# Weight products placed a unit at a time beside the heads of four attentions, and repeated products in the norms

## The chip, the cores and the metric

The kernel runs on one core of a Trainium2 chip. The metric is the device time of one execution in microseconds. All tensors are float32.

## The reference

A block with batch 1, 256 tokens and width 1,024, then a second one on its output. The first has two layers: latent attention (mla) and a full attention with a distance bias (moba, which with 256 tokens has a single key block), each followed by a residual sum, layer norm and a feed-forward layer with a three-tap convolution (width 2,816), again with residual sum and norm. The second has an attention mixer of two kinds (swa: a window with a sink and a bias table; fgt: a decaying attention), whose joined heads are gated, and a linear recurrence. Every normed input is scaled and shifted by a modulation vector that is computed from c. Cut to what matters:

```
for i in (0, 1):                                   # first block
    mod = silu(c) @ mod_w[i] + mod_b[i]            # 6 x 1024
    y = mixer_i(x * (1 + scale) + shift)           # mla, then moba: 8 heads of 128
    x = layer_norm(4 ** .25 * x + gate * y)
    y = conv_ffn(x * (1 + scale2) + shift2)
    x = layer_norm(4 ** .25 * x + gate2 * y)
for i in (0, 1):                                   # second block
    mod = silu(c_2) @ ada_w[i] + ada_b[i]          # 3 x 1024
    h = rmsnorm(x) * (1 + scale) + shift
    y = (concat(swa(h), fgt(h)) * silu(gate)) @ w_out   or   rglru(h)
    x = x + gate * y
out = rmsnorm(x)
```

## The kernel before, in words

Five engines each have a hand-written list of instructions, which meet in counted semaphores. Features lie on partitions and tokens in the free dimension, in tiles of 128 x 256.

**Weights.** `weight_stream` lists the chunks (128 x 2,048 elements, 1 MB) in the order of use. The sync engine fetches them into the ring `raw` of three chunks. A chunk is two *units* of 1,024 columns. For every unit ScalarE writes the rounded half `w_hi`, and then VectorE the remainder `w_lo = raw - w_hi`; both rings hold six units. The functions `ahead(u)` on both engines do this up to unit u, and `product(key)` does it up to five units beyond a chunk and then waits until TensorE has used the chunk (`w_used`). Each product is then three matmuls, hi x hi, hi x lo and lo x hi (`feature_product` with features out, `token_product` with tokens out). A unit is 24 matmuls of 256 columns or 12 of 512.

**Modulation.** GpSimd fetches 88 row blocks of `mod_w` and `ada_w_2` (`modulation`) into two slots `modraw`. VectorE's `modulate(n)` multiplies n of them by an element of silu(c) and adds them to an accumulator of 2,048 or 1,024 columns. `fold` on TensorE turns a finished accumulator, and on VectorE sums it.

**Attention.** Function `attention` on three engines. In turn t of before, TensorE makes the scores of head t, transposes the probabilities of head t-2 and makes the value product of head t-3. VectorE takes the maximum of head t's scores with mask or bias (L1622, L1624) and the shift (L1633), then the reciprocal of head t-1 (L1642) and o_lo of head t-4 (L1646), and at some turns a modulation step (L1404). ScalarE makes the exponentials of head t (L1073, L1075), normalises head t-1 (L1085, L1087), copies the transposed probabilities probT of head t-2 (L1096) and o_hi of head t-3 (L1102). No weight product stands in an attention; the next units are converted until the rings are full. Projections end before an attention begins, and the product with the output weights (`out_projection`, 8 units) begins after it. `swa` and `fgt` put two heads into one tile (`pair`).

**Norms.** Behind an output product, VectorE adds the four blocks to x (`block_sum`, L1476), VectorE and ScalarE make the statistics and scale x, TensorE turns it (`norm_turns`, L587) first for tokens 0 to 127 and then for the rest, and ScalarE evicts with the modulation. The norm between the first and the second block (layer 3 followed by rms norm, `layer_then_rms_norm`) needs the gain and offset rows, which `ln_rows(3)` has fetched into vv in the sixth iteration of the second feed-forward layer. GpSimd clears vv for swa's and fgt's values behind that norm (L495), beside VectorE's scaling of x (L1603).

Of the kernel before, what the change touches and what calls it, by code (L numbers as in the profile page):

```python
# [16 lines left out]
P = 128  # L17
D = 1024
KT = D // P
# [39 lines left out]
VZ = 10  # L59
# [56 lines left out]
def weight_stream(w):  # L116
# [35 lines left out]
    for part in range(3):  # L152
        for m in range(4):
            cols(("moba_in", part * 4 + m), w["moba_w_in"][0], part * 1024 + m * 256)
    rows2("moba_o", w["moba_w_o"][0])
    ffn(1)
    ain = w["attn_w_in_2"][0]
    cols(("a_kv", 0), ain, 512)
    cols(("f", 0), ain, 2304, 8, 2)
# [46 lines left out]
def build(nc, w, consts, out):  # L206
# [29 lines left out]
    with ExitStack() as ctx:  # L236
# [62 lines left out]
        def vtile(t, n, a=0, b=P):  # L299
# [15 lines left out]
        modacc = [of[:, :] if g in (3, 5, 7) else kk[:, 8 * S:12 * S] if g == 2 else  # L315
                  vv[:, 8 * S:12 * S] if g == 10 else modsum[:, :] for g in range(NG)]
# [13 lines left out]
        gain_row = [bias[:, 4 * S:8 * S], bias[:, 4 * S:8 * S], vv[:, 0:D], vv[:, 0:D]]  # L330
        offset_row = [vv[:, 0:D], kk[:, 8 * S:12 * S], vv[:, D:2 * D], vv[:, D:2 * D]]
# [57 lines left out]
        turn_keys = [("moba_in", i) for i in range(12)]  # L389
        turn_keys += [("a_kv", 0), ("f", 0)] + [(n, m) for n in ("a_q", "b_q", "b_k", "b_v") for m in range(2)]  # L390
        turn_keys += [("a_gate", m) for m in range(4)] + [("xr", m) for m in range(4)]
        turn_keys += [("l_gate", m) for m in range(4)]
        turn_of = {key: n for n, key in enumerate(turn_keys)}

# [51 lines left out]
        def _(pool):  # L446
# [31 lines left out]
            modulation(4 * KT, 7 * KT - 1)  # L478
            for h in range(2, HEADS):
                alibi_table(h)  # L480
                if h in (4, 7):
                    n = 7 * KT - 1 + (h - 4) // 3
                    modulation(n, n + 1)
            modulation(7 * KT + 1, 8 * KT)
            pool.wait_ge(sem("head_out"), 16)
            pool.wait_ge(sem("x_updated"), 2)
# [6 lines left out]
            modulation(8 * KT, 8 * KT + VZ)  # L493
            pool.wait_ge(sem("x_updated"), 4)
            pool.memset(vv[:, :], 0.0).then_inc(sem("vv_zero"), 1)  # L495
            modulation(8 * KT + VZ, len(mods))

# [8 lines left out]
        def _(pe):  # L506
# [18 lines left out]
            def columns_chunk(key, dst, a, width=256, e=None, heads=None):  # L525


                u0 = unit0(*key)
                step = min(width, P)
                for u in (u0, u0 + 1):  # L530
                    start_unit(u)
                    for k in range(4):
                        kt = 4 * (u - u0) + k
                        if e is not None:
                            pe.wait_ge(sem("h_ready"), 8 * e + kt + 1)
                        if heads is not None:
                            pe.wait_ge(sem("o_ready"), heads[kt])
                        for f in range(width // step):
                            at = k * width + f * step
                            ins = feature_product(dst[0:step, f * S:(f + 1) * S], u,  # L540
                                                  lambda r: r[:, at:at + step], tiles(a[0], kt, kt + 1),
                                                  tiles(a[1], kt, kt + 1), kt == 0 and f == 0, kt == KT - 1)
                    if u == u0:
                        ins.then_inc(sem("w_used"), 1)
                return ins

            def end_chunk(ins):
                ins.then_inc(sem("w_used"), 1)

            def turn(key):  # L550

                n = turn_of[key]
                if n >= 4:
                    pe.wait_ge(sem("turn_read"), n - 3)
# [1467 lines left out]
```

## Time and profile before

| | us |
|---|---|
| median of 3 runs (983.44 to 989.82) | 984.64 |
| the profiled execution | 988.01 |
| its span | 986.2 |
| TensorE matmul busy | 848.5 (86%) |
| VectorE busy | 743.2 (75%) |
| ScalarE busy | 518.5 (53%) |
| GpSimd busy | 74.4 (8%) |
| mean granted TensorE clock | 0.942 of 2.4 GHz |

The profiled execution took 1.8 us more than its span. Matmuls overlap in the records, so TensorE's work is read from the distance of their starts. Stages by the start of their products: mla's projections to 103, its attention to 135, mla_o to 158, first feed-forward layer 165 to 357, moba's projections to 437, attention to 466, moba_o to 489, second feed-forward layer 495 to 692, the second block's projections 711 to 769, swa and fgt to 821, gates and attn_o to 872, recurrence to the end.

### The profile page before, as it was taken

The page shows a single profiled execution, that of the slowest core. Times are in us where ns is not written, and L with a number is a line of the kernel's source. Part 1 is how long each engine was busy: PE and PEld are TensorE (multiplying, and loading weights), DVE is VectorE, ACT ScalarE, POOL GpSimd, SP SyncE. Part 2 cuts the span into 40 slices and gives each one's busy share as a digit, 9 for nine tenths or more (in the row PEclk, how much of TensorE's full clock was granted, in tenths as well). Part 3 has the DMA queues.
Part 4 walks back from the last instruction along what each step waited for, and adds up shares of the span by engine and source line. Part 5 has one row for each costly group of instructions (what it writes and reads, how often), then busy time and mean ns, then how long its engine had stood idle before and what let it go on. Part 6 is the DMA issues. An engine that isn't in the chain of part 4 may idle for free.

```text
span 986.2 us, 14678 instructions
## 1 busy us (share of the span) xinstructions
PE 848.5 (86%) x5608; PEld 775.1 (79%) x5608; DVE 743.2 (75%) x1153; ACT 518.5 (53%) x891; POOL 74.4 (8%) x118
## 2 busy tenths in 40 slices
PE   0387898999999989987899999999499789888946
PEld 0277677999999979976798998998399668778935
DVE  3889768787878778886688867767778655779684
ACT  0345656545445474447473535544555666464961
POOL 1000010010000000113000040000100000000100
PEclk9888999999999989997989999999699899999878
DMA  8877744778797739985457799865198511656411
GB/s 326 282 232 273 242 161 142 253 248 307 274 326 264 273 120 347 378 316 182 149 159 288 257 219 330 268 223 178 69 290 285 171 43 65 207 172 198 171 43 43
DMA packets 122677, 216.29 MB, mean 219 GB/s; under 512 B 12235, under 2 KB 97975, under 8 KB 115440
## 3 DMA queue, kind: packets, MB, share of 16 engines
q1 hardware_dynamic: 106828, 134.79, 40.7%
q0 software_dynamic: 12960, 72.46, 21.4%
q10 hardware_dynamic: 2820, 8.11, 2.5%
q8 instruction: 45, 0.74, 0.3%
q14 instruction: 24, 0.20, 0.1%
HBM read 214.18 MB, written 1.15 MB: 218 GB/s over the span
## 4 chain that ended last, share of the span: by engine, by line
PE 58%; DVE 21%; ACT 10%; DMA 5%; issue 5%; SPq 0%; DVEq 0%; ACTq 0%
PE bank L515 11%; PE bank L516 11%; PE bank L517 11%; PE bank L521 6%; PE bank L523 6%; PE bank L522 6%; DVE w_lo L1374 5%; DVE modsum L1404 3%; DMA raw<-in_ffn_w_in 2%; DMA raw<-in_mod_w 2%; ACT w_hi L938 2%; PE bank L570 1%; PE bank L616 1%; DVE of L1404 1%; PE bank L630 1%
## 5 line engine op out<-in xcount | busy, mean ns | idle before, releaser
L1374 DVE TENSOR_TENSOR w_lo<-raw,w_hi 128x1024 fp32r<-128x1024 f32 (+3 forms) x250 | 291.9, 1204 | 103.3 <-ACT w_hi L938 102.5
L515 PE MATMUL bank<-h_hi,w_hi 128*128 128x256 f32 (+2 forms) x1184 | 342.4, 289 | 10.4 <-DVE h_lo L1457 4.4
L516 PE MATMUL bank<-h_lo,w_hi 128*128 128x256 f32 (+2 forms) x1184 | 339.8, 287 | 0.0
L517 PE MATMUL bank<-h_hi,w_lo 128*128 128x256 f32 (+2 forms) x1184 | 339.6, 287 | 0.0
L938 ACT ACTIVATE w_hi<-raw 128x1024 fp32r<-128x1024 f32 (+3 forms) x250 | 250.1, 1031 | 132.2 <-PE bank L523 52.7
L515 PEld LDWEIGHTS bank<-h_hi,w_hi 128*128 128x128 f32 (+2 forms) x1184 | 231.1, 195 | 14.9 <-issue 11.2
L516 PEld LDWEIGHTS bank<-h_lo,w_hi 128*128 128x128 f32 (+2 forms) x1184 | 231.2, 195 | 1.4 <-issue 0.5
L517 PEld LDWEIGHTS bank<-h_hi,w_lo 128*128 128x128 f32 (+2 forms) x1184 | 231.0, 195 | 0.2
L521 PE MATMUL bank<-w_hi,o_hi 128*128 128x512 f32 x312 | 125.3, 402 | 13.0 <-DVE o_lo L1893 13.0
L522 PE MATMUL bank<-w_lo,o_hi 128*128 128x512 f32 x312 | 122.6, 393 | 0.0
L523 PE MATMUL bank<-w_hi,o_lo 128*128 128x512 f32 x312 | 122.5, 393 | 0.0
L1404 DVE SCALAR_TENSOR_TENSOR modsum<-modraw,small,modsum 128x2048 f32<-128x2048 f32 (+1 forms) x38 | 81.7, 2151 | 5.4 <-DMA modraw<-in_mod_w 2.8
L521 PEld LDWEIGHTS bank<-w_hi,o_hi 128*128 128x128 f32 x312 | 59.5, 191 | 26.0 <-issue 13.9
L523 PEld LDWEIGHTS bank<-w_hi,o_lo 128*128 128x128 f32 x312 | 59.1, 190 | 12.8
L522 PEld LDWEIGHTS bank<-w_lo,o_hi 128*128 128x128 f32 x312 | 59.4, 190 | 12.1 <-issue 0.7
L456 POOL DMA_DIRECT2D modraw<-in_mod_w x52 | 27.9, 538 | 386.8 <-DVE modsum L1404 135.9
L1123 ACT ACTIVATE kk<-kk 128x512 f32<-128x512 f32 x22 | 13.9, 632 | 69.9 <-DVE kk L1675 69.9
L456 POOL DMA_DIRECT2D modraw<-in_ada_w x32 | 17.1, 535 | 398.0 <-DVE modsum L1404 191.7
L1404 DVE SCALAR_TENSOR_TENSOR of<-modraw,small,of 128x2048 f32<-128x2048 f32 (+1 forms) x21 | 41.9, 1994 | 2.2 <-DMA modraw<-in_mod_w 0.6
L1129 ACT ACTIVATE o_hi<-kk 128x512 fp32r<-128x512 f32 x22 | 13.9, 632 | 45.5 <-DVE kk L1679 43.4
L1118 ACT ACTIVATE kk<-bank,cols 128x256 f32<-128x256 f32 x44 | 22.4, 560 | 26.5 <-PE bank L517 26.5
L616 PE MATMUL bank<-cst,prob 128*128 128x128 f32 x96 | 20.1, 327 | 18.2 <-ACT prob L1087 18.1
(271 smaller groups left out, 1132.5 us busy)
## 6 DMA issues: line engine op xcount, KB each, us to landing
raw<-in_ffn_w_in SPq DMA_DIRECT2D x88, 512.0 KB, 5.9
modraw<-in_mod_w POOLq DMA_DIRECT2D x36, 1024.0 KB, 6.3
raw<-in_ffn_w_out SPq DMA_DIRECT2D x44, 512.0 KB, 7.3
modraw<-in_ada_w POOLq DMA_DIRECT2D x16, 1024.0 KB, 5.6
raw<-in_attn_w_in SPq DMA_DIRECT2D x26, 512.0 KB, 5.7
raw<-in_moba_w_in SPq DMA_DIRECT2D x24, 512.0 KB, 8.9
modraw<-in_mod_w POOLq DMA_DIRECT2D x16, 512.0 KB, 4.3
modraw<-in_ada_w POOLq DMA_DIRECT2D x16, 512.0 KB, 5.0
```

The lines of the kernel that those rows point to most:

```text
L456: pool.dma_start(modraw[:, slot, at:at + src.shape[1]], src).then_inc(sem(f"mod_in{slot}"), 16)
L515: pe.matmul(dst, cut(hi(u)), a_hi, start=first, stop=False, skip_group_check=True)
L516: pe.matmul(dst, cut(hi(u)), a_lo, start=False, stop=False, skip_group_check=True)
L517: return pe.matmul(dst, cut(lo(u)), a_hi, start=False, stop=last, skip_group_check=True)
L521: pe.matmul(dst, a_hi, cut(hi(u)), start=first, stop=False, skip_group_check=True)
L522: pe.matmul(dst, a_hi, cut(lo(u)), start=False, stop=False, skip_group_check=True)
L523: return pe.matmul(dst, a_lo, cut(hi(u)), start=False, stop=last, skip_group_check=True)
L616: ins = pe.transpose(b[:, i * P:(i + 1) * P], prob[:, (g % SD) * CAUSAL + i * P:(g % SD) * CAUSAL + (i + 1) * P], ident)
L938: act.activation(hi(v), raw_unit(v), ACT.Copy).then_inc(sem("w_hi_ready"), 1)
L1118: act.activation(tiles(conv, s, s + 1), bank[0][:, t * S:(t + 1) * S], ACT.Identity, bias=cb[:, f:f + 1], scale=w2[:, 2 * FT + f:2 * FT + ...
L1374: dve.tensor_tensor(lo(v), raw_unit(v), hi(v).bitcast(F32), ALU.subtract).then_inc(sem("w_lo_ready"), 1)
L1404: ins = dve.scalar_tensor_tensor(acc, src, ck, acc, ALU.mult, ALU.add)
```

## The change

- `attention` on each engine takes a function `beside(t)`. The steps run to t = 9 with three heads in flight: TensorE makes the scores of head t+1 (head 0 stands ahead of the loop), the transposes of head t-1, the value product of head t-2, and then one weight unit. The units are those of `beside_units`: ukv 1 and mla_o 0 to 4 in mla; moba_in 9 to 11 and moba_o 0 to 3 in moba; b_q, b_k and b_v 0 in swa; a_gate 1 to 3 and attn_o 0 and 1 in fgt. Chunks are reordered for it (moba_in: q, k and v by pairs of heads; f ahead of a_kv), and PSUM banks are given by a table. The transposes use one bank (2) and the value products one (3), two each before.
- ScalarE's and VectorE's part of a step convert one unit (`ahead(units[t] + AHEAD)`) and evict what the unit two steps back has completed.
- Modulation steps that stood beside the projections stand in `after(t)` of VectorE's steps: mla ten (six in the attention before), moba five (three), swa four (none), fgt five (two). moba's four updates of x stand in its steps 0 to 3.
- `norm_turns` holds groups of 5 or 8 products of `o_hi` and `h_hi` into bank 0, whose result nobody reads (`keep_busy`), behind waits for the sums and statistics.
- The four gates of the second block are copied raw (`gate_raw`) and go through Silu together at step 7 of fgt.
- The rows of `ln_rows(3)` go to `of`, and are fetched in the last iteration of the second feed-forward layer. The clearing of vv stands ahead of the 16 bias DMAs, when x is updated for the third time.

```diff
@@ build: tables
+        beside_units = {
+            "mla": {t: unit0("ukv", 1) + t for t in range(2)} | {t: unit0("mla_o", 0) + t - 4 for t in range(4, 9)},
+            "moba": {t: unit0("moba_in", 9) + t for t in range(6)} | {t: unit0("moba_o", 0) + t - 6 for t in range(6, 10)},
...
-        gain_row = [bias[:, 4 * S:8 * S], bias[:, 4 * S:8 * S], vv[:, 0:D], vv[:, 0:D]]
+        gain_row = [bias[:, 4 * S:8 * S], bias[:, 4 * S:8 * S], vv[:, 0:D], of[:, 0:D]]
@@ gpsimd
             pool.wait_ge(sem("head_out"), 16)
-            pool.wait_ge(sem("x_updated"), 2)
+            pool.wait_ge(sem("x_updated"), 3)
+            pool.memset(vv[:, :], 0.0).then_inc(sem("vv_zero"), 1)
...
-            pool.wait_ge(sem("x_updated"), 4)
-            pool.memset(vv[:, :], 0.0).then_inc(sem("vv_zero"), 1)
@@ tensor
+            def keep_busy(count):
+                for _ in range(count):
+                    pe.matmul(bank[0][:, 0:S], o_hi[:, 0:P], tiles(h_hi, 0, 1), start=True, stop=True,
+                              skip_group_check=True)
             def norm_turns(n):
...
+                pe.wait_ge(sem("fold_summed"), fold_n[0])
+                keep_busy(5)
+                pe.wait_ge(sem("acc_read"), 4 * p + 3)
+                keep_busy(5)
+                pe.wait_ge(sem("acc_read"), 4 * p + 4)
+                keep_busy(5)
+                if n == 4:
+                    pe.wait_ge(sem("x_full"), 1)
+                    keep_busy(8)
+                    pe.wait_ge(sem("x_full"), 3)
+                    keep_busy(8)
                 for t in range(2):
+                    if t:
+                        pe.wait_ge(stage("offset_ready", n), 2 * order(n) + 2)
+                        keep_busy(5)
+                        pe.wait_ge(stage("rooted", n), 2 * order(n) + 2)
+                        keep_busy(5)
@@ tensor, moba
+            def moba_beside(t):
+                if t == 0:
+                    pe.wait_ge(sem("fold_summed"), fold_n[0])
+                if t < 6:
+                    turn_unit(("moba_in", 9 + t // 2), t % 2)
+                else:
...
+                    row_unit("moba_o", t - 6)
@@ vector, attention
+                for t in range(-1, HEADS + 2):
+                    h = t + 1
...
+                    beside(t)
+                    if t in units:
+                        ahead(units[t] + AHEAD)
+                    if h < HEADS:
                         dve.wait_ge(sem("exped"), 2 * g + 2)
...
+                    after(t)
@@ scalar, second feed-forward layer
-                    if l == 1 and i == 5:
-                        act.wait_ge(sem("x_updated"), 3)
+                    if l == 1 and i == FI - 1:
+                        act.wait_ge(sem("fold_turned"), parts_before[8])
                         ln_rows(3)
```

VectorE's rows of two turns of moba's attention before, the second with a modulation step (prob,stat<-bank,vv is the maximum, vv holding the bias; stat the shift and the reciprocal):

```order
L1622 ISA prob,stat<-bank,vv 128x128 [waits alibi,prob_turned,scores]
...
L1633 TENSOR_SCALAR stat<-stat 128x2 [waits row_max]
L1642 RECIPROCAL stat<-stat 128x2 [waits exped]
L1646 TENSOR_TENSOR o_lo<-bank,o_hi 128x256 [waits o_hi_ready]
L1404 SCALAR_TENSOR_TENSOR modsum<-modraw,small,modsum 128x2048 [waits mod_summed,mod_in0]
```

And of one step of it now:

```order
L1776 ISA prob,stat<-bank,vv 128x128 [waits alibi,prob_turned,scores]
L1776 ISA stat 128x1
L1778 ISA prob,stat<-bank,vv 128x256
L1778 ISA stat 128x1
L1787 TENSOR_SCALAR stat<-stat 128x2 [waits row_max]
L1527 TENSOR_TENSOR w_lo<-raw,w_hi 128x1024 [waits w_hi_ready]
L1797 RECIPROCAL stat<-stat 128x2 [waits exped]
L1801 TENSOR_TENSOR o_lo<-bank,o_hi 128x256 [waits o_hi_ready]
L1557 SCALAR_TENSOR_TENSOR modsum<-modraw,small,modsum 128x2048 [waits mod_summed,mod_in1]
```

The w_lo has moved in between the shift and the reciprocal, and the reciprocal, which was that of the head before, is now that of the same head.

ScalarE's rows of one turn in moba before:

```order
L1073 ACTIVATE prob,stat<-prob,stat 128x128 [waits shifted]
L1075 ACTIVATE prob,stat<-prob,stat 128x256
L1085 ACTIVATE prob<-prob,stat 128x128 [waits inverse_ready]
L1087 ACTIVATE prob<-prob,stat 128x256
L1096 ACTIVATE probT<-bank 128x384 [waits head_out,prob_turned]
L1102 ACTIVATE o_hi<-bank 128x256 [waits head_out]
```

And of one step now:

```order
L1180 ACTIVATE probT<-bank 128x384 [waits head_out,prob_turned]
L1187 ACTIVATE prob,stat<-prob,stat 128x128 [waits shifted]
L1189 ACTIVATE prob,stat<-prob,stat 128x256
L1043 ACTIVATE w_hi<-raw 128x1024 [waits w_used,w_in1_0]
L1201 ACTIVATE o_hi<-bank 128x256 [waits head_out]
L1213 ACTIVATE prob<-prob,stat 128x128 [waits inverse_ready]
L1215 ACTIVATE prob<-prob,stat 128x256
```

The w_hi copy has come in behind the exponentials, and the probT copy has moved ahead of them.

## Rows read from the trace of the kernel before

**Rows 1.** The page, the chain that ended last, shares by engine.
```profile
PE 58%; DVE 21%; ACT 10%; DMA 5%; issue 5%; SPq 0%; DVEq 0%; ACTq 0%
```

**Rows 2.** Timeline, TensorE in mla's projection: start us, us, engine line op out<-in.
```profile
56.47 0.28 PE L516 MATMUL bank<-h_lo,w_hi 128*128 128x256 f32 x1
56.59 0.28 PE L517 MATMUL bank<-h_hi,w_lo 128*128 128x256 f32 x1
```

**Rows 3.** Windows: stretch, us, then busy of PE, PEld, DVE, ACT, POOL, PEclk, DMA.
```profile
94.70:158.50 63.80, 54.71 (x277) 44.20 (x276) 49.77 (x114) 35.66 (x88) 5.83 (x11) 0.97 0.66 226
419.90:488.90 69.00, 59.65 (x336) 51.29 (x334) 49.17 (x101) 38.17 (x89) 12.18 (x12) 0.93 0.64 228
722.00:872.00 150.00, 135.50 (x902) 122.73 (x900) 102.56 (x229) 84.04 (x194) 6.36 (x12) 0.95 0.54 178
437.10:465.90 28.80, 19.48 (x88) 15.52 (x88) 20.97 (x62) 21.02 (x66) 11.12 (x10) 0.82 0.62 216
```

**Rows 4.** Timeline, VectorE and then ScalarE, one head of moba.
```profile
450.76 0.29 DVE L1622 CUSTOM_DVE_ANT_0 prob<-bank,vv 128x128 f32<-128x128 f32 x1 [2.29 <-PE bank L606]
...
451.44 0.17 DVE L1633 TENSOR_SCALAR stat<-stat 128x2 f32<-128x2 f32 x1
451.52 0.16 DVE L1642 RECIPROCAL stat<-stat 128x2 f32<-128x2 f32 x1
451.60 0.40 DVE L1646 TENSOR_TENSOR o_lo<-bank,o_hi 128x256 fp32r<-128x256 f32 x1
...
451.65 0.40 ACT L1073 ACTIVATE prob<-prob,stat 128x128 f32<-128x128 f32 x1 [0.88 <-DVE stat L1633]
...
452.45 0.19 ACT L1075 ACTIVATION_READ_ACCUMULATOR prob<-prob,stat 128x1 f32 x1
452.54 0.39 ACT L1085 ACTIVATE prob<-prob,stat 128x128 f32<-128x128 f32 x1
452.83 0.49 ACT L1087 ACTIVATE prob<-prob,stat 128x256 f32<-128x256 f32 x1
```

**Rows 5.** Groups by line: busy us, mean ns of one | idle before, releaser.
```profile
L1374 DVE TENSOR_TENSOR w_lo<-raw,w_hi 128x1024 fp32r<-128x1024 f32 (+3 forms) x250 | 291.9, 1204 | 103.3 <-ACT w_hi L938 102.5
L938 ACT ACTIVATE w_hi<-raw 128x1024 fp32r<-128x1024 f32 (+3 forms) x250 | 250.1, 1031 | 132.2 <-PE bank L523 52.7 <-PE bank L517 36.1 <-DMA raw<-in_moba_w_in 14.5
L1404 DVE SCALAR_TENSOR_TENSOR modsum<-modraw,small,modsum 128x2048 f32<-128x2048 f32 (+1 forms) x38 | 81.7, 2151 | 5.4 <-DMA modraw<-in_mod_w 2.8 <-PE bank L517 1.5 <-DVE lncol L1446 0.2
L1422 DVE TENSOR_REDUCE modc<-bank 128x4 f32<-128x512 f32 x24 | 15.7, 685 | 4.6 <-PE bank L570 4.5
```

**Rows 6.** Timeline, end of the second feed-forward layer, ScalarE and VectorE.
```profile
684.34 0.63 ACT L1129 ACTIVATE o_hi<-kk 128x512 fp32r<-128x512 f32 x1 [2.14 <-DVE kk L1679]
...
687.94 0.68 DVE L1476 TENSOR_TENSOR prob<-bank,grow 128x512 f32<-128x512 f32 x1
```

**Rows 7.** Timeline, ScalarE, evictions of the last ukv product.
```profile
103.20 1.08 ACT L1207 ACTIVATE kk<-bank 128x512 f32<-128x512 f32 x2 [1.70 <-PE bank L523]
```

**Rows 8.** Windows around the norms, and from the timeline TensorE in the second norm.
```profile
165.00:182.00 17.00, 17.00 (x133) 17.00 (x133) 14.36 (x24) 13.34 (x20) 0.00 (x0) 0.91 0.58 192
356.80:366.00 9.20, 5.75 (x26) 4.88 (x26) 5.99 (x21) 7.46 (x17) 0.00 (x0) 0.63 0.00 0
488.90:499.10 10.20, 7.08 (x34) 6.24 (x35) 6.99 (x21) 9.06 (x21) 0.00 (x0) 0.67 0.00 1
872.00:881.40 9.40, 6.35 (x36) 5.68 (x37) 6.29 (x15) 8.64 (x21) 0.00 (x0) 0.82 0.01 2
...
359.03 1.86 PE L587 MATMUL bank<-cst,x 128*128 128x128 f32 x8 [2.22 <-ACT x L988]
```

**Rows 9.** Timeline, the norm of layer 3, VectorE and GpSimd.
```profile
705.24 3.03 DVE L1603 TENSOR_SCALAR qz<-x,nstat 128x512 f32<-128x512 f32 x1
705.34 2.66 POOL L495 MEMSET vv<- 128x3072 f32 x1 [17.62 <-DVEq L1604]
```

**Rows 10.** DMA issues: engine, count, KB each, median us to landing.
```profile
vv<-in_ln_b ACTq DMA_DIRECT2D x3, 512.0 KB, 6.4
```

More of the change, by code:

```diff
@@ L523, in token_product, with columns_unit @@
                 return pe.matmul(dst, a_lo, cut(hi(u)), start=False, stop=last, skip_group_check=True)
-            def columns_chunk(key, dst, a, width=256, e=None, heads=None):
-                u0 = unit0(*key)
+            def columns_unit(key, i, dst, a, width=256, e=None):
+                u = unit0(*key) + i
                 step = min(width, P)
[L530 to L545, printed above, removed]
@@ L615, in attention @@
+            def attention(kind, scores, value, pair, beside):
+                h0 = HEAD[kind]
+                for t in range(HEADS + 2):
+                    if t + 1 < HEADS:
+                        score(kind, scores, t + 1)
+                    if 1 <= t <= HEADS:
+                        g = h0 + t - 1
+                        pe.wait_ge(sem("prob_ready"), g + 1)
+                        if t >= 2:
+                            pe.wait_ge(sem("probT_ready"), g)
                         for i in range(3):
-                            ins = pe.transpose(b[:, i * P:(i + 1) * P],
+                            ins = pe.transpose(bank[2][:, i * P:(i + 1) * P],
@@ L819, in _ @@
+            score("mla", mla_scores, 0)
+            attention("mla", mla_scores, mla_value, False, mla_beside)
             out_projection("mla_o", 2)
@@ L896, in _ @@
+            score("fgt", fgt_scores, 0)
+            attention("fgt", fgt_scores, lambda h, t: vtile(t, 4 + h), True, fgt_beside)
             out_projection("attn_o")
@@ L1288, in _, with mixed_high @@
                 sem("lam_exp"), 1)
[L1289 to L1295 removed]
+            for m in range(2):
+                product("b_v", m)
+                b_out("b_v", m)
+            def mixed_high(m):
                 act.wait_ge(sem("head_gated"), m + 1)
@@ L1773, in _, with rotate @@
                 sem("kr_ready"), 1)
-            for j in range(2):
-                product("uq", j)
-                modulate(1)
+            def rotate(j):
                 dve.wait_ge(sem("q_swapped"), j + 1)
@@ L1810, in _ @@
             layer_norm(1)
-            for i in range(12):
+            for i in range(9):
                 product("moba_in", i)
@@ L1886, in _ @@
+            attention("fgt", True, causal, after=fgt_after)
+            mixed(3)
+            o_low(of, 2, 16)
+            o_low(of, 3, 16)
             dve.wait_ge(sem("lam_exp"), 1)
```

749 lines of the change are left out of this document (421 added, 328 removed).

## The prediction

> **What bounds the kernel now.** I read the page first, then the busy time by stage, then the order of instructions of one head. The chain that ended last is TensorE's for 58% and VectorE's for 21% [rows 1]. So TensorE sets the end over most of the program, and the reader is to ask where it waits. Its work there is weight products: a 256-column product follows the one before after 0.12 us [rows 2] (56.59 less 56.47), so a unit of 24 takes 2.87 us and a chunk of two 5.73. In the feed-forward layers that is the whole story, and the change leaves them alone. It moves things in three stretches [rows 3]: mla from the end of its second query product to the end of mla_o (63.8 us), moba from the end of chunk 8 to the end of moba_o (69.0), and from the first a_q chunk to the end of attn_o (150.0). In moba's attention itself TensorE is busy 19.5 of 28.8 us, at 0.82 of its clock [rows 3]: there is a hole of some 9 us there and others like it, and the change wants them filled with units.
>
> What sets the pace in a filled hole? One head on the other two engines [rows 4]: VectorE's maximum and shift run from 450.76 to 451.61, 0.85 us; ScalarE's two exponentials start 0.04 later and end at about 452.60, 0.95 us; the reciprocal is 0.16, the normalisation to 453.32 is 0.78, o_lo 0.40. A weight unit needs a w_hi copy of 1.03 us on ScalarE and then a w_lo subtraction of 1.20 us on VectorE, and a wide modulation step is 2.35 (the mean of 2.15 mixes widths) [rows 5].
>
> **A step of the new order.** TensorE's share of a step is one score (0.7 us with one operand pair, 1.3 with two), three transposes (0.35), a head's value product (0.65) and a unit (2.87): 4.5 us in moba and swa, 5.15 in mla and fgt. The first three are estimates from the columns at the pace of rows 2, four times that pace for the unrounded operands. The new VectorE order, though, is: maximum of head t+1; w_lo; reciprocal of the same head; o_lo; modulation. The w_lo waits for the w_hi of the same step, and ScalarE makes that only behind the exponentials of head t+1, which wait for the maximum. Nothing in this overlaps: 0.85 + 0.04 + 0.95 + 1.03 + 1.20 + 0.16 and some 0.07 of hand-overs = 4.3 us, 4.7 with o_lo, and 7.05 with a wide modulation step. Before, a head's reciprocal came behind the next head's maximum and no weights were converted among them, so that the two engines overlapped. The normalisation (0.78) and the probT copy run on ScalarE under VectorE's modulation and cost nothing; without a modulation they fit just under o_lo and the next maximum. TensorE may be a step ahead, but its transposes wait for the probabilities, so it goes at this ring's pace in nearly every step. The units then do fill the holes, and the steps grow.
>
> moba, counted from the end of chunk 8: modulation 2.35 and head 0 (0.85 + 0.95 + 0.3) 4.5; steps 0 to 3 each 4.7 and an update of x of 1.2 (1,024 columns, as w_lo), without o_lo in two, 22.8; steps 4 to 6 at 7.05, 21.2; sum 48.5. Then o_lo of head 5 (1.20 + 0.40) 50.1, modulation and o_lo of head 6 (3.95) 54.05, the last value product and its unit (3.5) 57.6, the fold 0.9 and four units 11.5: 70.0. The score that now stands ahead of chunk 8 adds 0.7. 70.7 against 69.0: **+1.7**.
>
> mla, from 94.7: VectorE reaches head 0 at 100.6, since it has the distance table (2.1) and three modulation steps first. Head 0 2.1; step 0 6.65; step 1 6.7 (the rotation, three 512-column operations of 0.7 [rows 6], lies beside the exponentials); step 2 5.6 (four evictions of 0.55 [rows 7] ahead of o_hi); step 3 6.6 (four folds of 0.65 to 0.69 [rows 5]); steps 4 to 6 6.0, 7.3, 6.0 with narrow modulation of 1.29. That is 147.5; o_lo of heads 5 and 6, the last modulation, the fold and three units (8.5) as in moba end at 163.0. 68.3 against 63.8: **+4.5**.
>
> From 722.0: what stands ahead (below) makes it 1.5 late; VectorE's logarithm, spreads and w_lo bring it to the first swa head 18.1 after 722.0. A swa step has four small instructions more (0.6) and a bias row (0.33): 5.2, or 7.55 with a modulation; head 0 and seven steps take 47.8, and TensorE's tail (7.4) ends at 71.4. Two chunks 11.5, gating of the first pair 2.6: 85.5. fgt: head 0 2.1, steps at 4.3 and 6.65 by turns, 2.0: 122.4. The fold 2.6, two steps with a unit 7.5, six units 17.2: 149.7, and 0.5 for mixing. 150.2 against 150.0: **+0.2**.
>
> **The clock inside the steps.** TensorE will stand still for 1.5 to 2.5 us in most steps. The stretch of moba's attention shows 0.82 with such holes [rows 3]; a stretch at 1.2 GHz makes a step's 4.5 us of TensorE up to 8. Mostly this disappears in the ring's 6 to 7 us, some of it at the tails doesn't. The bounds are 0 and 8 us; I take **+2**, as most of the 27 steps are longer than TensorE's share even with half of it slowed.
>
> **The norms.** Repeated products stand in TensorE's waits. Around the norms the granted clock was 0.63 over 9.2 us, 0.67 over 10.2 and 0.82 over 9.4, and 0.91 in the 17 us behind the first [rows 8]: at the level of 1.2 GHz for 6.8, 6.7, 3.4 and 3.1 us. Ahead of the fall at the second norm TensorE had stood still for 2.2 us [rows 8]. What it did in that time would take half as long at 2.4 GHz, and part of it is paced by the evictions: at most 1.7 + 1.9 + 2.8 + 1.7 = 8.1 us to be had. The repeated products themselves (5 x 0.12 = 0.6 us each set) end before what the transposes wait for: nothing, at worst 0.6 per norm. I take **-6.5**, with bounds of -8 and +2. By the Trainium skill (TensorE: Matmul & The Clock Gate, "What's actually happening") the halved clock is the default state and activity is what lifts it; the trace agrees in that the clock fell behind idle time alone, but no row shows whether products worth nothing count.
>
> **The norm of layer 3.** The memset of vv moves away from beside VectorE's scaling of x. That scaling took 3.03 us while the memset took 2.66 [rows 9]; a 512-column operation near it takes 0.7 [rows 6]. So 2.3 us go. The Trainium skill (SBUF — State Buffer, its rule on the shared port pair) calls this an exclusive lock, in which the later one waits the other out; the row agrees (3.03 is about 2.66 and the operation), and by it the memset will hold up one VectorE operation in the feed-forward layer instead, under TensorE. But the gain and offset rows are now fetched at the end of that layer, behind the last o_hi copy (684.97 [rows 6]), and such a fetch landed after 6.4 us [rows 10]: 691 or so, and VectorE, which now starts on the sum at 687.94 and is busy from there to the end, waits 3.0. At the old clock the sets between the transposes add about 1, a full clock takes it back, and the first chunk is now f, which runs as fast as h comes. Together 1.5 late at 722, which the third stretch has in it.
>
> Sum: 4.5 + 1.7 + 0.2 + 2.0 - 6.5 = **+1.9 us**. The profiled execution took 988.0 us (span 986.2), 0.3% above the median of 984.6; on the median it gives 986.5.
>
> **The rivals.** (a) The steps overlap after all and each is as long as its fullest engine: VectorE alone 5.0 with modulation, TensorE 4.5 or 5.15 without. That is 1.3 to 2 us less in 27 steps, about 40 us: 946. For it speaks that the stretches hold only some 52, 54 and 126 us of TensorE work; against it, w_lo waits for a w_hi behind the exponentials in the same step. (b) The other side: the clock. If the hole in each step holds TensorE at 1.2 GHz, a step is 4.5 x 1.8 = 8 us and not 6 to 7, from the point at which more than half of a step is at the low level: 1 to 1.5 us in some 12 steps without wide modulation, more at the tails, 18 in all, and with no more than 2 us from the norms: 984.6 + 6.4 + 18 - 2 = 1007. (c) The repeated products don't hold the clock: 6.5 less gained, 993.
>
> **How the numbers follow.** Forecast 0.48 (980 to 993), (c) 0.15, (b) 0.17, (a) 0.20 with what lies between it and the forecast. A measurement of this kernel tells about 1% (9.8 us). Faster by over 1% (below 974.8): 0.20. Slower (above 994.5): (b) and a fifth of (c), 0.20. Within: 0.60. The range from 966 to 1000 leaves out about half of (a) and of (b).
>
> **What would show it.** In the changed profile: VectorE in a moba step idle before w_lo for about 2 us, released by w_hi; steps of 5.9 and 7.05 us; the three stretches at 71, 68 and 150 us; the clock at 1.0 around three norms; the scaling of x at 0.6 us; the first sum of layer 3's norm waiting for a DMA of the rows. It is wrong if the steps are under 5 us, or if the clock inside them stays at the low level.

## The result, and the profile after

| | before | changed |
|---|---|---|
| median, us | 985.96 (983.44 to 989.82) | 998.99 (997.54 to 1000.67) |
| ratio, 95% interval | | 1.0126 (1.0102 to 1.0149) |
| profiled execution, its span | 988.01, 986.2 | 999.93, 998.1 |
| TensorE matmul busy | 848.5 | 856.6 |
| VectorE busy | 743.2 | 739.2 |
| ScalarE busy | 518.5 | 522.4 |
| mean granted TensorE clock | 0.942 | 0.959 |

The change makes the kernel 1.3% slower, although TensorE's clock is higher. The busy times say little: the work of VectorE and ScalarE is the same, and what grew is waiting. The chain that ended last, shares by engine, shows whose waiting:

```profile
PE 49%; DVE 26%; ACT 12%; issue 8%; DMA 4%; SPq 0%; DVEq 0%; ACTq 0%
```

TensorE's share fell from 58% [rows 1] to 49% and VectorE's rose from 21% to 26%. The group of w_lo, of the changed kernel (busy us, mean ns of one, then the idle time ahead of it and what ended it):

```profile
L1527 DVE TENSOR_TENSOR w_lo<-raw,w_hi 128x1024 fp32r<-128x1024 f32 (+2 forms) x250 | 292.3, 1205 | 139.1 <-ACT w_hi L1043 138.7
```

Its idle time went from 103.3 [rows 5] to 139.1 us: VectorE waits 36 us more for w_hi.

The three stretches, changed kernel (start and end, us, then busy time of PE, PEld, DVE, ACT, POOL, the granted clock, DMA share, GB/s), as [rows 3]:

```profile
95.33:164.44 69.11, 55.49 (x278) 45.61 (x278) 49.69 (x109) 35.63 (x88) 6.36 (x12) 0.93 0.60 209
425.83:496.74 70.91, 58.24 (x335) 50.60 (x334) 48.67 (x101) 38.50 (x89) 10.30 (x12) 0.90 0.62 220
735.51:883.75 148.24, 131.32 (x904) 121.10 (x903) 101.59 (x228) 86.75 (x197) 6.36 (x12) 0.98 0.53 178
```

Cut at the same products in both traces, the 11.9 us come from these places (from the first to the last product of each stretch, us; the norms are numbered from 0, and the norm of layer 3 is numbers 3 and 4):

| stretch | before | changed | difference | forecast |
|---|---|---|---|---|
| start to end of second query product | 94.73 | 95.33 | +0.6 | 0 |
| mla to the end of mla_o | 63.72 | 69.11 | +5.4 | +4.5 |
| moba from chunk 0 to the end of chunk 8 | 55.8 | 56.4 | +0.6 | in moba |
| moba to the end of moba_o | 69.0 | 70.91 | +1.9 | +1.7 |
| norms 0, 1, 2, 5 and the first products behind them | | | -1.75 | -6.5 |
| norm of layer 3 | 18.42 | 21.03 | +2.6 | +1.5 with the next |
| f, a_kv and the fold | 11.42 | 14.01 | +2.6 | |
| a_q to the end of attn_o | 149.97 | 148.24 | -1.7 | -1.3 |
| rest of the feed-forward layers and the recurrence | | | +1.7 | 0 |
| clock inside the steps | | | in the stretches | +2 |

**A step.** VectorE, and then ScalarE, in one step of moba, changed kernel (start us, us, engine, line, operation, out<-in, in brackets the idle time before it and its releaser), as [rows 4]:

```profile
435.52 0.29 DVE L1776 CUSTOM_DVE_ANT_0 prob<-bank,vv 128x128 f32<-128x128 f32 x1
...
436.20 0.17 DVE L1787 TENSOR_SCALAR stat<-stat 128x2 f32<-128x2 f32 x1
438.37 1.23 DVE L1527 TENSOR_TENSOR w_lo<-raw,w_hi 128x1024 fp32r<-128x1024 f32 x1 [2.00 <-ACT w_hi L1043]
439.52 0.16 DVE L1797 RECIPROCAL stat<-stat 128x2 f32<-128x2 f32 x1
439.59 1.21 DVE L1703 TENSOR_TENSOR x<-x,bias 128x1024 f32<-128x1024 f32 x1
440.83 0.29 DVE L1776 CUSTOM_DVE_ANT_0 prob<-bank,vv 128x128 f32<-128x128 f32 x1
...
436.41 0.40 ACT L1187 ACTIVATE prob<-prob,stat 128x128 f32<-128x128 f32 x1 [0.83 <-DVE stat L1787]
...
437.30 1.04 ACT L1043 ACTIVATE w_hi<-raw 128x1024 fp32r<-128x1024 f32 x1
439.71 0.40 ACT L1213 ACTIVATE prob<-prob,stat 128x128 f32<-128x128 f32 x1 [1.37 <-DVE stat L1797]
```

Read across the engines, only one of the two works at a time up to the reciprocal: VectorE's shift until 436.37, ScalarE's exponentials and w_hi until 438.34, VectorE's w_lo and reciprocal until 439.7. The step is 5.31 us long (435.52 to 440.83), and VectorE idles 2.00 of them ahead of w_lo.

What TensorE does meanwhile, changed kernel, where moba turns to its output product:

```profile
463.45 0.67 PE L679 MATMUL bank<-probT,vv 128*128 128x256 f32 x2 [1.98 <-DVE o_lo L1801]
463.96 0.38 PE L681 MATMUL bank<-probT,vv 128*128 128x128 f32 x2
468.91 0.80 PE L529 MATMUL bank<-w_hi,o_hi 128*128 128x512 f32 x1 [4.56 <-ACT vv L1353]
469.50 0.63 PE L530 MATMUL bank<-w_lo,o_hi 128*128 128x512 f32 x1
```

It is ahead of the other two, stands still 4.56 us for the eviction of the last v (which ScalarE makes behind the exponentials of head 7 and the w_hi), and then runs most of that unit at 1.2 GHz (granted clock 0.56): 468.91 to 474.04, 5.1 us for what takes 3.0 in unit_first below.

### The profile page after: what moved, and what is told of

It is laid out like the page before. It is cut to its first block, busy times and chain, and to the rows that moved or that the text cites. A ratio compares the mean times of both kernels' runs of the same rounds, so it can differ in the third digit from the quotient of the medians.

```text
span 998.1 us, 14975 instructions
## 1 busy us (share of the span) xinstructions
PE 856.6 (86%) x5749; PEld 785.6 (79%) x5749; DVE 739.2 (74%) x1153; ACT 522.4 (52%) x896; POOL 72.5 (7%) x118
## 4 chain that ended last, share of the span: by engine, by line
PE 49%; DVE 26%; ACT 12%; issue 8%; DMA 4%; SPq 0%; DVEq 0%; ACTq 0%
PE bank L523 9%; PE bank L524 9%; PE bank L525 9%; DVE w_lo L1527 6%; PE bank L529 6%; PE bank L531 6%; PE bank L530 6%; DVE modsum L1557 4%; ACT w_hi L1043 4%; DMA raw<-in_mod_w 2%; DMA raw<-in_ffn_w_in 2%; ACT prob L1189 1%; PE bank L595 1%; ACT kk L1110 1%; DVE of L1557 1%
## 5 line engine op out<-in xcount | busy, mean ns | idle before, releaser
L1527 DVE TENSOR_TENSOR w_lo<-raw,w_hi 128x1024 fp32r<-128x1024 f32 (+2 forms) x250 | 292.3, 1205 | 139.1 <-ACT w_hi L1043 138.7
L1043 ACT ACTIVATE w_hi<-raw 128x1024 fp32r<-128x1024 f32 (+2 forms) x250 | 249.2, 1029 | 87.4 <-PE bank L525 27.2
L523 PEld LDWEIGHTS bank<-h_hi,w_hi 128*128 128x128 f32 (+2 forms) x1184 | 229.7, 194 | 25.7 <-issue 18.1
L529 PE MATMUL bank<-w_hi,o_hi 128*128 128x512 f32 x312 | 127.5, 409 | 17.6 <-DVE o_lo L2061 13.0
L1557 DVE SCALAR_TENSOR_TENSOR modsum<-modraw,small,modsum 128x2048 f32<-128x2048 f32 (+1 forms) x45 | 90.6, 2014 | 6.1 <-DMA modraw<-in_mod_w 3.0
L679 PE MATMUL bank<-probT,vv 128*128 128x256 f32 x64 | 21.6, 421 | 22.6 <-ACT of L1206 10.3
```

What stands on the lines that cost most here:

```text
L523: pe.matmul(dst, cut(hi(u)), a_hi, start=first, stop=False, skip_group_check=True)
L529: pe.matmul(dst, a_hi, cut(hi(u)), start=first, stop=False, skip_group_check=True)
L679: pe.matmul(dst, value(h, 0), pt[:, 0:S], start=not (pair and h % 2), stop=False, skip_group_check=True)
L1043: act.activation(hi(v), raw_unit(v), ACT.Copy).then_inc(sem("w_hi_ready"), 1)
L1527: dve.tensor_tensor(lo(v), raw_unit(v), hi(v).bitcast(F32), ALU.subtract).then_inc(sem("w_lo_ready"), 1)
L1557: ins = dve.scalar_tensor_tensor(acc, src, ck, acc, ALU.mult, ALU.add)
```

## The experiments

Each was run beside the kernel before; the ratio is to that. The rival theories of the first four: the steps go at the pace of a serial ring (maximum, exponentials, w_hi, w_lo and reciprocal one behind the other), or TensorE's single banks set them; the full clock in the norms is worth nothing, or 6.5 us; and the rows of layer 3 are waited for, or not.

**unit_first.** ScalarE's `attention`, all four kinds:

```
+                    if t in units:
+                        ahead(units[t] + AHEAD)
                     if t + 1 < HEADS:
                         g = h0 + t + 1
...
                         act.wait_ge(sem("shifted"), g + 1)
...
-                    if t in units:
-                        ahead(units[t] + AHEAD)
                     beside(t)
```

> The changed kernel with one edit: in all four attentions ScalarE makes the w_hi of a step ahead of the exponentials instead of behind them; the same work, on every engine. Ring theory (the steps go at the pace of maximum, exponentials, w_hi, w_lo, reciprocal in series): the 1.03 us of w_hi leaves the ring and w_lo (1.20) lies beside the exponentials (0.95), so that a moba step falls from 5.3 to 5.6 us to TensorE's share of 4.7, one with a wide modulation from 6.7 to 5.0, a swa step with a modulation from 7.3 to about 5.2; VectorE no longer idles 2 us ahead of w_lo; 15 to 20 us off in all, 979 to 984. Rival (the steps are held by TensorE's single banks for transposes and value products, which wait for o_lo and probT): the order on ScalarE changes nothing but where it idles, 0 to -3 us, 996 to 999.

Measured: 969.55 us, ratio 0.9821 (0.9784 to 0.9857), 29 us under the changed kernel and 1.8% under the kernel before. The same step of VectorE as above, and ScalarE's w_hi:

```profile
427.50 0.29 DVE L1776 CUSTOM_DVE_ANT_0 prob<-bank,vv 128x128 f32<-128x128 f32 x1
...
428.53 1.48 DVE L1527 TENSOR_TENSOR w_lo<-raw,w_hi 128x1024 fp32r<-128x1024 f32 x1 [0.19 <-ACT w_hi L1043]
429.93 0.15 DVE L1797 RECIPROCAL stat<-stat 128x2 f32<-128x2 f32 x1
430.01 1.20 DVE L1703 TENSOR_TENSOR x<-x,bias 128x1024 f32<-128x1024 f32 x1
431.24 0.29 DVE L1776 CUSTOM_DVE_ANT_0 prob<-bank,vv 128x128 f32<-128x128 f32 x1
...
427.45 1.05 ACT L1043 ACTIVATE w_hi<-raw 128x1024 fp32r<-128x1024 f32 x1
428.40 0.39 ACT L1189 ACTIVATE prob<-prob,stat 128x128 f32<-128x128 f32 x1
```

w_hi runs while VectorE takes the maximum, w_lo beside the exponentials, the wait is 0.19 and the step 3.74. The windows of the three stretches:

```profile
94.31:157.43 63.12, 53.28 (x278) 44.24 (x278) 49.72 (x109) 35.64 (x88) 6.33 (x12) 0.95 0.67 228
418.82:478.03 59.21, 53.27 (x334) 47.35 (x334) 49.52 (x101) 38.01 (x89) 11.98 (x12) 1.00 0.74 264
716.13:849.18 133.05, 126.60 (x904) 118.43 (x903) 101.60 (x228) 86.58 (x197) 6.34 (x12) 1.00 0.60 199
```

6.0, 11.7 and 15.2 us less than in the changed kernel, on nearly the same busy times of VectorE and ScalarE. (This profiled execution, 966.0 us, is the fastest of the four.) TensorE now sets the pace: its scores in moba start at 438.08, 442.59 and 447.10, 4.51 apart, which is its share of a step as the prediction had it. The banks are what they were, so the rival falls. The gain was larger than the 15 to 20 expected, because more went than the steps of VectorE: its seven steps in moba take 28.7 instead of 37.3, 8.6 of the 11.7. The other 3 are TensorE's long wait at the turn to the output product (4.56, now 3.39) and the unit at half clock behind it (5.1, now 3.0). In mla the ring is not the whole story: of the four steps with a unit two fall (6.30 to 5.36, 5.61 to 3.73) and two do not (6.34, now 6.26; 7.00, now 7.24), and no run settles what holds those two.

**plain_norms.** The changed kernel, `keep_busy`:

```
-                for _ in range(count):
+                for _ in range(0):
```

> The changed kernel without the repeated products (the waits in front of them stay; nothing of the computation is left out). Theory A (what the clock costs in the norms lies behind VectorE's and ScalarE's evictions): the granted clock falls again around four norms, but the time from the last output product to the first product behind the norm stays within 0.3 us, the 192 products behind norms 0 and 2 take 24.8 to 24.9 us instead of 24.4, and in the norm of layer 3 the ten products that stood at half clock between the transposes (2.2 us) are gone, so that the first product there comes 1.5 to 2 earlier: 997 to 999 us, no change. Theory B (the full clock is worth 6.5 us, and something else cost more): 1004 to 1006 us.

Measured: 999.05 us, ratio 1.0118 (1.0084 to 1.0152); against the changed kernel's 1.0126, no difference. The norm of layer 3 takes 21.00 us and not 21.04, so the 1.5 to 2 us expected there don't show. Its trace has the reason: the offset row landed 8.7 us after its issue (7.3 in the changed kernel), and VectorE waited 6.46 us for it and not 4.99. From VectorE's scaling of x to the first product behind the norm it is 3.18 us, and 4.68 in the changed kernel: that is the 1.5.

**before_busy.** The kernel before, `norm_turns`, with `keep_busy` and its seven calls as in the change.

> The kernel before with the repeated products alone added to its norms, at the same places and counts. Theory A: norms 0, 1, 2 and 5 give 1.5 us in all and the norm of layer 3 takes 0 to 1: 984 to 986, no change. Theory B: 978 to 980.

Measured: 984.92 us, ratio 0.999 (0.9966 to 1.0014). From the end of the output product to the first product behind norms 1 and 2, four kernels: before, changed, plain_norms, before_busy (columns as above; the granted clock is the third number from the end):

```profile
356.81:364.08 7.27, 3.83 (x16) 2.96 (x17) 4.61 (x17) 5.54 (x12) 0.00 (x0) 0.66 0.00 0
488.87:495.30 6.43, 3.29 (x17) 2.44 (x17) 3.80 (x13) 5.34 (x12) 0.00 (x0) 0.77 0.00 1
```

```profile
362.41:369.43 7.02, 5.38 (x42) 4.61 (x41) 4.62 (x17) 5.54 (x12) 0.00 (x0) 1.00 0.00 0
496.74:502.88 6.14, 5.03 (x41) 4.55 (x41) 3.81 (x13) 5.30 (x12) 0.00 (x0) 1.00 0.01 2
```

```profile
362.05:369.38 7.33, 3.10 (x16) 2.44 (x17) 4.61 (x17) 5.54 (x12) 0.00 (x0) 0.84 0.00 0
496.43:502.88 6.45, 3.11 (x17) 2.44 (x17) 3.80 (x13) 5.30 (x12) 0.00 (x0) 0.79 0.01 2
```

```profile
357.92:364.94 7.02, 5.39 (x43) 4.63 (x41) 4.61 (x17) 5.54 (x12) 0.00 (x0) 1.00 0.01 2
489.35:495.53 6.18, 5.21 (x41) 4.59 (x41) 3.80 (x13) 5.34 (x12) 0.00 (x0) 1.00 0.00 1
```

With the repeated products the clock is at 1.00, without them at 0.66 to 0.84, and these two norms are 0.25 to 0.3 us shorter. The 192 products behind norm 2 take 24.4 instead of 25.0. In norm 1 the second eight transposes and the first product behind them, before and then changed:

```profile
361.80 1.97 PE L587 MATMUL bank<-cst,x 128*128 128x128 f32 x8 [0.91 <-DVE x L1541]
364.08 0.55 PE L515 MATMUL bank<-h_hi,w_hi 128*128 128x256 f32 x1 [0.31 <-DVE h_lo L1527]
```

```profile
367.40 1.09 PE L634 MATMUL bank<-cst,x 128*128 128x128 f32 x8 [0.18 <-DVE x L1694]
369.43 0.35 PE L523 MATMUL bank<-h_hi,w_hi 128*128 128x256 f32 x1 [0.94 <-DVE h_lo L1680]
```

The transposes take 0.88 us less, and the wait for VectorE's h_lo behind them 0.63 more: what TensorE wins it mostly waits away. In before_busy's trace the four norms and what follows them give 1.7 us, and the norm of layer 3 with the 72 products behind it another 1.6 (11.42 became 10.04 there). Nearly all of it is lost again in the second feed-forward layer, which takes 199.5 us and not 196.9 although it begins 0.6 faster: a wait near its middle is 4.14 and not 2.13; ahead of it ScalarE's w_hi stood 4.73 us for the fetch of a weight chunk, and 2.85 in the kernel before. One trace doesn't tell whether that is chance. So the full clock is worth between nothing and some 3 us here, and Theory B (978 to 980) is out: its ratio, at most 0.995, lies outside the interval.

**rows_early.** The changed kernel, ScalarE's `ffn`:

```
-                    if l == 1 and i == FI - 1:
+                    if l == 1 and i == FI - 2:
                         act.wait_ge(sem("fold_turned"), parts_before[8])
                         ln_rows(3)
```

> The changed kernel with the gain and offset rows of layer 3 fetched one iteration of the second feed-forward layer earlier (about 17 us), where the accumulator in their place has just been turned. Theory (VectorE idles 5.0 us ahead of the first sum of that norm for the rows): the idle time is gone, the sum starts when TensorE has finished its first block, 4.2 us ahead of the end of the layer's products, so 3.2 us off: 994.5 to 996. Rival (the rows were there and the sum waits for TensorE's block): no change, 998 to 1000.

Measured: 996.11 us, ratio 1.0097 (1.0067 to 1.0128). VectorE at the start of that norm, in the changed kernel and then in rows_early:

```profile
694.30 0.22 DVE L1527 TENSOR_TENSOR w_lo<-raw,w_hi 128x64 fp32r<-128x64 f32 x1
699.50 0.69 DVE L1629 TENSOR_TENSOR prob<-bank,grow 128x512 f32<-128x512 f32 x1 [4.99 <-DMA of<-in_ln_b]
```

```profile
695.21 0.22 DVE L1527 TENSOR_TENSOR w_lo<-raw,w_hi 128x64 fp32r<-128x64 f32 x1
696.76 0.69 DVE L1629 TENSOR_TENSOR prob<-bank,grow 128x512 f32<-128x512 f32 x1 [1.33 <-PE bank L531]
```

The wait of 4.99 us for the rows is gone, and one of 1.33 for TensorE's block is left. From the last product to the first behind the norm it is 17.65 us and not 21.03: 3.4, against 3.2 expected. The stretch of f and a_kv is shorter too, 12.65 and not 14.01, at a granted clock of 1.00 and not 0.88. Part is lost again: the third stretch takes 149.54 us and not 148.24.

**mod_first.** VectorE's modulation in moba, swa and fgt (steps 0, 2, 4) is called in `beside(t)`, ahead of `ahead(...)`, and no longer in `after(t)`:

```
+            def moba_before(t):
+                if 4 <= t < 9:
+                    modulate(1)
             def moba_after(t):
                 if 0 <= t < 4:
                     update(1, t)
-                if 4 <= t < 9:
-                    modulate(1)
```

> The changed kernel with VectorE's modulation steps of moba, swa and fgt (steps 0, 2, 4) ahead of the w_lo of their step instead of behind its reciprocal; ScalarE's order untouched. Ring theory: the 2.35 us (moba, swa, fgt) fill the 2.0 us in which VectorE waits for exponentials and w_hi, so that only the steps with a modulation get shorter: moba's from 6.7 to 5.0, swa's from 7.3 to 5.4, fgt's from 6.6 to 4.7 or TensorE's 5.1; the others stay at 5.3 to 5.6, 5.0 and 4.1. 9 to 13 us off: 986 to 990. Rival (unit_first won because ScalarE's evictions and TensorE's operands come sooner, not by a ring through VectorE): less than 3 us off, 996 to 999.

Measured: 982.65 us, ratio 0.996 (0.9942 to 0.9977), 16 us under the changed kernel. VectorE in a moba step with a modulation, where w_lo waits for nothing any more:

```profile
456.67 0.17 DVE L1787 TENSOR_SCALAR stat<-stat 128x2 f32<-128x2 f32 x1
456.75 2.35 DVE L1557 SCALAR_TENSOR_TENSOR modsum<-modraw,small,modsum 128x2048 f32<-128x2048 f32 x1
459.02 1.22 DVE L1527 TENSOR_TENSOR w_lo<-raw,w_hi 128x1024 fp32r<-128x1024 f32 x1
```

The steps, start of one maximum to the next: moba's without a modulation stay at 5.31, 5.30, 5.64 and 5.64, those with one fall from 6.65 and 6.73 to 4.56 and 4.69; swa's from 7.28 to 5.02, while its others stay at 5.01; in fgt, where TensorE's share is next, the seven steps take 29.3 us and not 34.2. Only what stood outside VectorE's wait got shorter, by what fits into it. That is a second cut through the same ring, on the other engine. The gain was larger than the 9 to 13 expected: moba's steps gave 4.1 us, swa's 5.7 and fgt's 4.9, and TensorE's wait at the turn to moba's output product fell from 4.56 to 2.37, which the expectation had left out.

**f_exp_late.** The changed kernel, ScalarE's eviction of a_kv ahead of the exponential of |f|:

```
-            act.wait_ge(sem("f_abs"), 1)
-            act.activation(prob[0:16, 2 * S:3 * S], prob[0:16, S:2 * S], ACT.Exp, scale=-1.0).then_inc(
-                sem("f_exp"), 1)
             b = turned(("a_kv", 0))
             act.activation(tiles(kk, 8, 10), b[:, :], ACT.Copy).then_inc(sem("turn_read"), 1)
+            act.wait_ge(sem("f_abs"), 1)
+            act.activation(prob[0:16, 2 * S:3 * S], prob[0:16, S:2 * S], ACT.Exp, scale=-1.0).then_inc(
+                sem("f_exp"), 1)
```

> The changed kernel with ScalarE's exponential of |f| behind a_kv's eviction instead of ahead of its conversions. Theory: ScalarE waits 2.8 us there for VectorE's |f|, which stands behind four w_lo, and the next w_hi comes only behind it; without it TensorE's 72 products of f and a_kv and the fold end some 2 us sooner: 996 to 997.5. Rival (TensorE is held by w_lo on VectorE, which has four in a row to make anyway): no change, 998 to 1000.

Measured: 999.52 us, ratio 1.0137 (1.0114 to 1.016). No gain: the stretch from f to a_q takes 14.08 us instead of 14.01. ScalarE's wait was not what TensorE waited for. My theory of this stretch fell.

**akv_first.** The changed kernel with a_kv ahead of f in the stream and on every engine:

```
-    cols(("f", 0), ain, 2304, 8, 2)
     cols(("a_kv", 0), ain, 512)
+    cols(("f", 0), ain, 2304, 8, 2)
```

> The changed kernel with a_kv ahead of f again, in the weights' order and on all engines. Theory (with f first, VectorE's w_lo among the first eight h_lo copies behind the norm of layer 3 is a full one of a_kv, 1.22 us, where it was f's narrow one, 0.22; TensorE stands still 1.36 us for the sixth tile of h and runs the next ones at half clock): the wait of 1.36 us goes and the 72 products and the fold take 11.4 to 11.9 us instead of 14.0: 996 to 998. Rival (the stretch is held by the four w_hi and w_lo in a row behind the h copies, in either order): 13.5 to 14 us there, 998 to 1000.

Measured: 996.51 us, ratio 1.0101 (1.008 to 1.0121). VectorE among the h copies in the changed kernel, and its TensorE:

```profile
723.45 1.22 DVE L1527 TENSOR_TENSOR w_lo<-raw,w_hi 128x1024 fp32r<-128x1024 f32 x1
...
725.48 0.28 PE L523 MATMUL bank<-h_hi,w_hi 128*16 128x256 f32 x1 [1.36 <-DVE h_lo L1680]
```

The same place on VectorE in akv_first, and the window from a_kv to a_q:

```profile
722.39 0.22 DVE L1527 TENSOR_TENSOR w_lo<-raw,w_hi 128x64 fp32r<-128x64 f32 x1
...
720.45:730.49 10.04, 10.04 (x76) 8.74 (x77) 8.95 (x18) 9.28 (x17) 0.00 (x0) 1.00 0.54 176
```

14.01 us became 10.04, more than the 2.1 to 2.6 expected. The wait of 1.36 is gone, and so is the time at 1.2 GHz (granted clock 0.88 in the changed kernel, 1.00 here): at 0.88 the clock was low for some 3.4 of 14.01 us, which costs about 1.7 by my estimate. The remaining 0.9 is not explained. The execution as a whole gained 2.5 us: the norm ahead was 0.7 longer and the third stretch 1.5, so that part of these 4 us was lost again. plain_norms and rows_early show the same: they too come to the first a_q chunk 2.4 and 3.8 us sooner, and their third stretch takes 149.5 and not 148.2. No run shows what takes it back.

**Combinations.** `combined` is unit_first, rows_early and f_exp_late, without repeated products in the norm of layer 3; `combined_mod` adds mod_first, `combined_akv` akv_first as well.

> unit_first with the rows of layer 3 fetched an iteration earlier, the exponential of |f| late, and no repeated products in the norm of layer 3. If the four terms add: 969.6 - 3.2 - 2 - 1.5 = 962 to 964, 2.2% under the kernel before. If they overlap, 965 to 967.

> The combined kernel with the modulation ahead of w_lo as well. With w_hi ahead of the exponentials VectorE no longer waits there, so the modulation has no idle time to fill and stands ahead of w_lo and reciprocal in its step: by the ring theory no gain, and up to 3 us lost, 962 to 966. If the modulation's place were worth something in itself: 955 to 960.

> combined_mod with a_kv ahead of f. The same two theories: 1 to 1.5 us off by the first (in the combined kernels that stretch takes 12.65 us, not 14.0), 959 to 960; by the second no change, 960 to 961.5.

| | us | ratio to before |
|---|---|---|
| combined | 962.70 | 0.9764 (0.9739 to 0.9788) |
| combined_mod | 960.61 | 0.9739 (0.9718 to 0.976) |
| combined_akv | 960.02 | 0.9729 (0.9705 to 0.9753) |

combined lies in the range expected if four terms add (962 to 964), but not by those terms: f_exp_late had given nothing of its 2 us. Against unit_first its norm of layer 3 takes 15.73 us and not 20.77, and f with a_kv 12.66 and not 14.03, 6.4 us in all, and here the third stretch gives nothing back (133.09 against 133.05). rows_early alone has 17.65 and 12.65 there, so that leaving out the repeated products of that norm is worth 1.9.

The modulation's place is worth nothing that can be told once w_hi has left the ring: the intervals of combined and combined_mod overlap. 960.61 is also neither in the range of the ring theory (962 to 966) nor in the rival's (955 to 960), so that this run decides nothing between them. All three are over 2.3% faster than the kernel before; which of them is best is not settled, since they differ by less than their intervals. In combined_akv the stretch of f and a_kv again takes 10.04 us and not 12.65, and the median falls by only 0.6, which fits both theories.

## Why the prediction was right or wrong

It said 986.5 us, between 966 and 1000, with no clear change as the likeliest. The time is 999.0, at the edge of that range, and slower by more than 1%, to which I had given 0.20. On the profiled execution it is +11.9 and not +1.9. That the time lies inside owes more to the width of the range than to the sum: the range was drawn for the rivals (a) and (b), and neither came about. The 10 us between the two are 4.75 for the norms, 3.7 for the norm of layer 3 and f, 2.3 for what was not foreseen and 1.3 for the three stretches, less the 2 for the clock.

- **A step of the new order: right.** The ring of maximum, exponentials, w_hi, w_lo and reciprocal is there, with its 2 us of idle time on VectorE, and two independent cuts through it shorten the steps that they should: mod_first in moba, swa and fgt, unit_first there and in two of four such steps of mla. Nearly all steps were 0.2 to 0.4 us shorter than forecast: in moba 5.31, 5.31, 5.63, 5.64, 6.65 and 6.73 against 5.5, 5.5, 5.9, 5.9 and 7.05 (my durations overlap by some 0.08 at each hand-over within an engine); in mla 6.30, 6.34, 5.95, 6.55, 5.61 and 7.00 against 6.65, 6.7, 5.6, 6.6, 6.0 and 7.3; in swa 5.01 and 7.28 against 5.2 and 7.55; in fgt 4.10 and 6.62 against 4.3 and 6.65.
- **The stretches: right in kind, a little low.** mla +5.4 against +4.5, and moba with the head that now stands ahead of chunk 8 +2.5 against +1.7, in spite of the shorter steps. What was missing in the forecast is TensorE's tails: it stands still for 4.56 us and starts the output product at half clock, which I had as 3.5 for the last value product and its unit.
- **The clock inside the steps (+2): no term of its own.** It fell as expected. But two like steps of VectorE in moba are 5.63 and then 5.64 us, and beside the second TensorE's unit took 4.4 us at 0.67 of the clock (446.72 to 451.09) instead of 3.1. Only at a tail does it count: 2.1 us in moba. It lies in the stretches.
- **The norms (-6.5): the step that failed.** Measured -1.75. I took the low level of 6.8, 6.7, 3.4 and 3.1 us and halved it, on the ground that what TensorE did there would take half as long, with only a part taken off for the evictions. That holds for a TensorE that sets the pace. There it waited for VectorE and ScalarE: norms 1 and 2 got 0.25 and 0.29 us shorter, norm 0 stayed and norm 5 took 0.26 more; the 192 products behind norms 0, 2 and 5 took 0.4, 0.6 and 0.5 less, those behind norm 1 the same. That the clock can be held by products worth nothing was right for these norms. By the Trainium skill (TensorE: Matmul & The Clock Gate, "What's actually happening") activity releases the throttle. The rows agree, and show that products whose result nobody reads count: 0.66 became 1.00. So rival (c), that the products don't hold the clock, named the wrong cause for nearly the right price.
- **The norm of layer 3 and f (+1.5): mis-sized.** +5.2. The wait for the rows was 4.99 and not 3.0: their fetch began at 691.9 and took 7.3 us for the offset row, and VectorE came to its scaling of x 16.4 us after the last product and not 13.1. The memset's 2.3 us did go, the scaling took 0.49 us and not 3.03, but the ten repeated products between the transposes ran mostly at half clock (granted clock 0.57) and took most of that time up:

```profile
715.84 1.97 PE L634 MATMUL bank<-cst,qz 128*128 128x128 f32 x8 [0.81 <-ACT qz L1095]
717.46 2.22 PE L602 MATMUL bank<-h_hi,o_hi 128*128 128x256 f32 x10
719.52 1.04 PE L634 MATMUL bank<-cst,qz 128*128 128x128 f32 x8
```

  In plain_norms the sixteen transposes and what lies between take 3.65 us, here 4.7. From the scaling to the first product it was 5.36 us before, 4.68 here and 3.18 in plain_norms, so the repeated products cost 1.5 where I had set what they cost against a full clock; combined against rows_early says 1.9. Of the memset's row I said that it agrees with a lock in which the later one waits. By their starts the scaling was the earlier one (705.24 against 705.34), and yet it was the one held up. And of f I said that it "runs as fast as h comes": what was behind it I had not looked at. The stream's order also sets which w_lo falls among the h copies (akv_first), 2.6 us.
- **The third stretch** (+0.2, with 1.5 brought along): -1.7 against -1.3 by itself, right, but with an error in its working. Behind swa 18.1, 47.8 and 7.4 make 73.3 and not 71.4; with 73.3 the forecast would have been +0.6 by itself. In mla, how 147.5 becomes 163.0 is not written out and can't be redone from the terms.
- **Not foreseen:** +0.6 ahead of mla, +1.3 in the second feed-forward layer, where a wait of 2.1 us near its middle became 3.6, and 0.4 at the end. These were not tested. Ahead of mla the unchanged code took 94.31 us in unit_first and 94.76 in mod_first, so that the 0.6 may be chance. The wait in the layer goes back to the fetch of a weight chunk, for which ScalarE's w_hi stood 6.17 us and not 2.85. It was 2.6 in combined_akv and 4.1 in before_busy, and over the twelve traces that layer takes 196.6 to 199.5 us, so that this too may be chance.
- **Rival (a)**, each step as long as its fullest engine, did not hold for the change and gave 946 us. It describes the steps of unit_first in moba and swa, which came to 970.
- **Rival (b)**, the other side, had the right sign and 1007 us, but another cause: it wanted TensorE to set the steps at half clock, and VectorE's steps did not change with that clock (5.63 and 5.64).

## What to carry to other kernels

When work for a starved engine is put into a loop of two other engines, write out the order of those two side by side: here one copy on the wrong side of the exponentials made them wait for each other, cost 29 us, and turned a gain of 1.8% into a loss of 1.3%. The change as a whole was good; the place of w_hi on ScalarE was not. In the norms here a low clock cost little, because TensorE waited there for the others; so before pricing a low clock look at what ends TensorE's waits. Extra products that run at the low clock can themselves delay what stands behind them. And a tile that is fetched later because its place was taken needs its landing time checked against its first reader.

## What the runs showed of the hardware that was not expected

- In the norm of layer 3 the sets of 5, 13 and 8 repeated products stood behind waits of 2.9, 3.8 and 2.1 us. The set of 13 ran at a granted clock of 0.50 and that of 8 at 1.00, but the first transposes, behind a further wait of 0.8, ran at 0.50 as in the kernel before. In the other norms, with 15 products within 2 to 2.7 us and 10 later, the clock stayed at 1.00.
- The memset of 2.68 us that had lengthened VectorE's scaling from 0.49 to 3.03 us cost nothing in its new place (574.39 to 577.07): beside it stood two modulation steps, 4.81 us for both, and three w_lo, 3.49 for the three, all at their usual pace. The prediction had it hold up one VectorE operation there. The Trainium skill (SBUF — State Buffer, "SBUF: two separate sides") limits the lock for a VectorE operation with two SBUF inputs to a GpSimd operation that reads SBUF. A memset reads nothing, so the two rows agree with that, and I had read the rule too broadly.
- A w_lo of 1,024 columns and GpSimd's distance table of moba hinder each other, and which one loses more goes by who starts first. In unit_first, where the table started 0.10 us ahead (428.43), it took its usual 1.17 us and w_lo 1.48 instead of 1.22. Where w_lo started 0.17 us ahead (436.25), w_lo took its usual 1.22 and the table 2.07:

```profile
436.25 1.22 DVE L1527 TENSOR_TENSOR w_lo<-raw,w_hi 128x1024 fp32r<-128x1024 f32 x1
436.42 2.07 POOL L484 TENSOR_SCALAR vv<-bias 128x384 f32<-128x384 f32 x1 [3.08 <-DVE stat L1787]
```
